# Hybrid attention and mixture-of-experts block: one flat loop of visits, quarter-form steps, the lone expert second

## The reference

```python
def _moe_ffn(h, w_router, w_gate, w_up, w_down):
    logits = h @ w_router
    top_val, top_idx = lax.top_k(logits, 2)
    gate = jax.nn.softmax(top_val, axis=-1)
    ...
    # for each token and each of its two experts e, with weights of width 3584:
    y_assign = (silu(x @ w_gate[e]) * (x @ w_up[e])) @ w_down[e]
    ...
    # the two results of a token, scaled by gate, are added up
```

## Time and profile before

| | us |
|---|---|
| median of 3 runs (1669.82 to 1673.24) | 1670.78 |
| the profiled execution | 1672.14 |
| its span on the core | 1670.4 |
| PE busy | 1544.0 (92%) |
| DVE busy | 418.1 (25%) |
| ACT busy | 250.2 (15%) |

### The profile page before, as it was taken

The page is one execution under the profiler, slowest core; times in us unless marked ns, Lnnn a source line. Parts: engine busy times, 40 slices in busy tenths (PEclk is TensorE's granted clock), DMA queues, the critical chain, the costliest instruction groups (busy, mean ns, idle before and its releaser), DMA issues.

```text
span 1670.4 us, 21757 instructions
## 1 busy us (share of the span) xinstructions
PE 1544.0 (92%) x8696; PEld 852.4 (51%) x8697; DVE 418.1 (25%) x955; ACT 250.2 (15%) x560; POOL 0.2 (0%) x4
## 2 busy tenths in 40 slices
PE   5988889999989998599999999999999999999996
PEld 2777658777657774444444443443333443333332
DVE  2366525333344533600002000110000300003003
ACT  2132210000012331110101010011111111111112
POOL 0000000000000000000000000000000000000000
PEclk8999799999999998799999999999999999999998
DMA  9974525765656440068979797999999999997991
GB/s 348 380 266 164 189 101 192 273 252 202 227 193 229 172 178 16 1 264 332 407 289 407 284 408 294 408 374 405 408 407 407 407 377 407 407 408 296 367 377 78
DMA packets 168185, 484.43 MB, mean 290 GB/s; under 512 B 10024, under 2 KB 20544, under 8 KB 168000
## 3 DMA queue, kind: packets, MB, share of 16 engines
q1 hardware_dynamic: 168128, 483.70, 75.8%
HBM read 482.63 MB, written 1.05 MB: 290 GB/s over the span
## 4 chain that ended last, share of the span: by engine, by line
PE 79%; DMA 9%; DVE 5%; SPq 3%; ACT 2%; issue 2%; DVEq 0%; ACTq 0%
PE bank L1024 11%; PE bank L931 9%; PE bank L1064 8%; DMA ring<-in_w_exp_up 8%; PE bank L778 7%; PE bank L1008 6%; PE bank L1185 6%; PE bank L1020 5%; PE bank L949 4%; PE bank L912 4%; PE bank L1058 3%; PE bank L1211 3%; PE bank L772 3%; SPq L629 2%; PE bank L1280 2%
## 5 line engine op out<-in xcount | busy, mean ns | idle before, releaser
L1024 PE MATMUL bank<-ring,hT 128*64 128x448 f32 x1280 | 255.1, 546 | 32.2 <-DMA ring<-in_w_exp_up 12.7
L1024 PEld LDWEIGHTS bank<-ring,hT 128*64 128x64 f32 x1280 | 89.0, 137 | 190.7 <-issue 153.7
L931 PE MATMUL bank<-hT,ring 128*128 128x256 f32 x704 | 158.0, 385 | 1.7 <-DVE hT L1429 1.7
L778 PE MATMUL bank<-hT,ring 128*128 128x256 f32 x640 | 153.0, 396 | 3.9 <-ACT hT L1953 2.5
L1809 DVE TENSOR_TENSOR bt<-arena,bank 64x512 f32<-64x512 f32 (+2 forms) x36 | 24.3, 675 | 493.5 <-PE bank L1024 249.6
L931 PEld LDWEIGHTS bank<-hT,ring 128*128 128x128 f32 x704 | 135.2, 193 | 24.1 <-issue 3.8
L778 PEld LDWEIGHTS bank<-hT,ring 128*128 128x128 f32 x640 | 124.5, 198 | 26.0 <-DVE hT L1429 4.4
L1064 PE MATMUL bank<-ring,bt 128*32 128x256 f32 (+1 forms) x1232 | 136.8, 445 | 0.0
L1348 DVE SCALAR_TENSOR_TENSOR acc<-ring,cond,acc 128x512 f32<-128x512 f32 x140 | 105.2, 752 | 4.9
L1020 PE MATMUL bank<-ring,hT 128*128 128x448 f32 x256 | 100.7, 546 | 4.1 <-DMA ring<-in_w_exp_up 3.4
L1008 PE MATMUL bank<-ring,hT 128*32 128x448 f32 x1024 | 102.8, 542 | 0.0
(11 more groups left out here) (279 smaller groups left out, 1179.8 us busy)
## 6 DMA issues: line engine op xcount, KB each, us to landing
ring<-in_w_exp_gate SPq DMA_DIRECT2D x128, 896.0 KB, 9.2
ring<-in_w_exp_up SPq DMA_DIRECT2D x128, 896.0 KB, 13.0
ring<-in_w_exp_down SPq DMA_DIRECT2D x64, 1536.0 KB, 15.9
ring<-in_w_ada SPq DMA_DIRECT2D x24, 2048.0 KB, 9.4
ring<-in_w_in SPq DMA_DIRECT2D x10, 2048.0 KB, 12.8
ring<-in_w_exp_down SPq DMA_DIRECT2D x32, 512.0 KB, 16.3
ring<-in_w_ff_gate SPq DMA_DIRECT2D x5, 2048.0 KB, 12.4
ring<-in_w_ff_up SPq DMA_DIRECT2D x5, 2048.0 KB, 12.8
```

The source lines that it names most:

```text
L778: last = mm(o[:, 0:T], w[:, k, t * P:(t + 1) * P], hT[:, k, :], start=(k == 0), stop=(k == KC - 1))
L931: last = mm(bank[n % 2][:, a * T:(a + 1) * T], w[a][:, k, t * P:(t + 1) * P], hT[:, k, :], start=(k == 0), stop=(k == KC - 1))
L1024: last = mm(o[64 * c2:64 * c2 + 64, 64 * c2:64 * c2 + EH], xsT[:, k, t0:t0 + 64], w[:, k, c2 * EH:(c2 + 1) * EH], start=(k == 0), stop=(k ...
```

## The change

Seven edits:

- **One loop.** The nested loops become one of NV = 21 visits. A visit is at most one small job, at most one large job behind it, and perhaps an end. Each engine reads five values per visit from the constant table (`job_at`, `ends_seen`, `has_small`, `large_no`, `end_of`), and inside the visit the class of its small or large expert.
- **Tiny steps.** A class 0 of up to 32 tokens (`TINY`). A small step of this class is one quarter unit: 32 matmuls for gate and up together, whose pieces are released as they are used; then Silu, product, four transposes and 28 down matmuls.
- **Order.** The smallest rank goes to position 2, and `LONE = 1`: the second large expert is the one alone. Jobs 0 to 11 keep their pattern, jobs 12 to 15 are `(3,0)` to `(3,3)`, then four pairs `(6,s) (5,s)` and four pairs `(8,s) (7,s)`.
- **Start.** Only the first half of the gather stands ahead of the loop. The second half, the first large window, the clearing of `ys`, `yacc` and banks 4 to 6, and the transposes of the scatter weights form an "end 3" behind job 0.
- **Scatter.** The first scatter (behind job 5) uses both tiles instead of one.
- **Small outputs.** For a class 0 expert the output is copied by four copies of 32 rows, two on each engine, instead of two of 64 rows, and DVE and ACT read the class for it.
- **Routing.** One more DVE instruction for the class, one that keeps the class of the other path at 1 or above.

The visits are (number of the job, small, large, end): `0 s end3; 1 L; 2 s; 3 s+L; 5 s end1; 6 s+L; 8 s; 9 s+L; 11 s end2; 12 L; 13 L; 14 L; 15 L end2; 16, 18, 20 s+L; 22 s+L end2; 24, 26, 28 s+L; 30 s+L end2`.

```diff
-STREAM_AT = (0, 1, 3, 5, 7, 2, 4, 6)
+STREAM_AT = (0, 1, 3, 5, 7, 6, 8, 2)
 NPOS = 16
-LONE = 3
+LONE = 1
 JOBS = []
 for l_ in range(4):
     for s_ in range(ES):
-        small_ = {0: 2 * (s_ // 2), 1: 4, 2: 6}.get(l_)
+        small_ = {0: 2 * (s_ // 2), 2: 6, 3: 8}.get(l_)
         if l_ != LONE:
             JOBS.append((small_, 2 * s_ % ES if l_ == 0 else s_))
         JOBS.append((2 * l_ + 1, s_))
         if l_ == 0:
             JOBS.append((small_, 2 * s_ % ES + 1))
-AHEAD_OF_LARGE = [n - 1 for n, (pos_, _) in enumerate(JOBS) if pos_ % 2]
-ENDS_SEEN = [0, 0, 1, 1] + [2] * 4 + [3] * 4 + [4] * 4
-JOBS_DONE = [12, 20, 28, 32]
+JOBS_DONE = [12, 16, 24, 32]
+VISITS = []
+small_left, ends_, j_ = ES, 0, 0
+while j_ < len(JOBS):
+    has_, large_ = JOBS[j_][0] % 2 == 0, 0
+    visit_ = [j_, ends_, int(has_), 0, 0]
+    j_ += has_
+    small_left -= has_
+    end_ = 3 if has_ and j_ == 1 else int(has_ and ends_ == 0 and small_left == 0)
+    end_ = 2 if has_ and j_ in JOBS_DONE else end_
+    if not end_ and j_ < len(JOBS) and JOBS[j_][0] % 2:
+        visit_[3] = JOBS[j_][0] // 2 + 1
+        j_ += 1
+    if not end_ and (j_ == len(JOBS) or j_ in JOBS_DONE):
+        end_ = 2
+    visit_[4] = end_
+    ends_ += end_ in (1, 2)
+    VISITS.append(visit_)
+NV = len(VISITS)
+PLAN = [v[0] for v in VISITS] + [len(JOBS)] + [v[k] for k in range(1, 5) for v in VISITS]
+NPLAN = len(PLAN)
+C_END = C_PLAN + NPLAN
 TX = 3 * P // 2
+SECOND_BANKS = (4, 5, 6, 1)
...
+TINY = 32
+UNITS = {0: [("quarter", 0)], 1: [("half", 0)], 2: [("half", 0), ("quarter", 64)], 3: [("wide", 0), ("quarter", 128)],
...
+        def large_class(eng, no):
+            return eng.value_load(route_i.rearrange("p a r -> p (a r)")[0:1, bass.ds(2 * no + 4 * NPOS - 1, 1)], min_val=0, max_val=4)
+
+        def planned(eng, at, u, most):
+            return eng.value_load(plan_i[0:1, bass.ds(u + at, 1)], min_val=0, max_val=most)
+
+        def job_at(eng, u):
+            return planned(eng, 0, u, 32)
+
+        def ends_seen(eng, u):
+            return planned(eng, NV + 1, u, 4)
+
+        def has_small(eng, u):
+            return planned(eng, 2 * NV + 1, u, 1)
+
+        def large_no(eng, u):
+            return planned(eng, 3 * NV + 1, u, 4)
+
+        def end_of(eng, u):
+            return planned(eng, 4 * NV + 1, u, 3)
...
-            for h in range(2):
+            def gather(h, banks):
+
                 pe.wait_ge(sel_v, 2 + h)
                 for k in range(KC):
                     for b in range(2):
-                        last = mm(bank[4 * h + k // 2][:, k % 2 * T:(k % 2 + 1) * T], xn[:, b, k * P:(k + 1) * P],
+                        last = mm(bank[banks[k // 2]][:, k % 2 * T:(k % 2 + 1) * T], xn[:, b, k * P:(k + 1) * P],
                                   sel[:, b, h * T:(h + 1) * T], start=(b == 0), stop=(b == 1))
                     if k % 2:
                         last.then_inc(gat_p, 1)
+
+            gather(0, range(4))
...
-            def quarter(t0, ks):
+            def quarter(t0, ks, alone=False):
 
                 for k in ks:
                     for q, w in enumerate((eg, eg, eu, eu)):
@@ -1009,6 +1043,8 @@
                                   w[:, k, (q % 2) * EH:(q % 2 + 1) * EH], start=(k == 0), stop=(k == KC - 1))
                         if k % 2 and q % 2:
                             last.then_inc(u_used if q == 3 else g_used, 1)
+                        elif alone and k == KC - 2 and q % 2:
+                            last.then_inc(eu_p if q == 3 else eg_p, 3)
...
+            def tiny_step(J, ends):
+
+                pe.wait_ge(xsS_v, ends + 1)
+                pe.wait_ge(yacc_v, 4 * ends + 12)
+                for k in range(0, KC, 2):
+                    pe.wait_ge(full_g[k // 2], 16 * J + 16)
+                    pe.wait_ge(full_u[k // 2], 16 * J + 16)
+                    quarter(TX, range(k, k + 2), True)
+                pe.wait_ge(yzS_v, ends + 1)
+                pe.wait_ge(eh_v, 4 * J + 4)
+                h, one_ = hs[64:P, 0, :], ident[64:P, 64:P]
+                mm(bank[3][:, 0:64], h[:, 0:P], one_, start=True, stop=True)
+                for t in range(1, 4):
+                    last = nc.tensor.transpose(bank[3][:, t * 64:(t + 1) * 64], h[:, t * P:(t + 1) * P], one_)
+                last.then_inc(et_p, 4)
+                down(J, 0, 0, ALL, (0,), 7)
...
-                pe.wait_ge(xsS_v, 1)
-                turn_scatter_weights(0, bank[3])
-                with nc.Fori(0, 4, engines=PE, head_slot={PE[0]: 0}) as l:
-                    which = class_at(pe, 2 * l + 1)
-                    with pe.Fori(0, ES) as i:
-                        J = job_ahead(pe, l, i)
-                        ends = ends_seen(pe, l, i)
-                        with pe.If(l != LONE):
+                with nc.Fori(0, NV, engines=PE, head_slot={PE[0]: 0}) as u:
+                    J, ends, has, large, end = (f(pe, u) for f in (job_at, ends_seen, has_small, large_no, end_of))
+                    with pe.If(has != 0):
+                        tiny = class_at(pe, 2 * ends)
+                        with pe.If(tiny == 0):
+                            tiny_step(J, ends)
+                        with pe.Else():
                             small_step(J, ends)
+                    with pe.If(large != 0):
+                        which = large_class(pe, large)
                         with pe.If(which == 3):
-                            large_step(l, J + 1, ends, 3)
+                            large_step(large, J + has, ends, 3)
                         with pe.Else():
-                            large_step(l, J + 1, ends, 2)
-                        with pe.If(l == 0):
-                            small_step(J + 2, ends)
-                            with pe.If(i == 1):
-                                stream_scatter(0, (1,))
-                    stream_scatter(l + 1, (0, 1))
+                            large_step(large, J + has, ends, 2)
+                    with pe.If(end != 0):
+                        with pe.If(end == 3):
+                            gather(1, SECOND_BANKS)
+                            turn_scatter_weights(0, bank[0])
+                            pe.wait_ge(sgt_a, 1)
+                        with pe.Else():
+                            stream_scatter(ends, (0, 1))
             with pe.Else():
+                gather(1, range(4, 8))
                 with nc.Fori(0, NE, engines=PE, head_slot={PE[0]: 0}) as r:
                     pe.wait_ge(xsT_v, r + 1)
                     which = class_of(pe, r)
@@ -1656,8 +1713,8 @@
                 signal(ins, sel_v)
 
...
-            then(ts(total, sums, float(CAPS[0]), 1.0, ALU.is_gt, ALU.add))
-            for cap in CAPS[1:]:
+            then(ts(total, sums, float(TINY), None, ALU.is_gt))
+            for cap in CAPS:
...
+                with ve.If(class_at(ve, 2 * g) == 0):
+                    for c in (2, 3):
+                        last = nc.vector.tensor_copy(ys[64:96, 1, c * T:(c + 1) * T], bank[7][32 * c:32 * c + 32, 0:T])
+                    last.then_inc(ys_v, 1)
+                with ve.Else():
+                    nc.vector.tensor_copy(ys[64:P, 1, CW:D], bank[7][64:P, :]).then_inc(ys_v, 1)
...
-                stream_weights(0)
                 gathered(0)
                 small_window(None)
-                gathered(1)
-                large_window(1)
-                ve.wait_ge(sgt_p, 1)
-                stream_weights(1)
-                signal(nc.vector.memset(ys, 0.0), dv)
-                nc.vector.tensor_copy(yacc, xs[:, :, :]).then_inc(yacc_v, 4 * NE + 1 - 20)
-                for i in (4, 5, 6):
-                    last = nc.vector.memset(bank[i][:, :], 0.0)
-                last.then_inc(yzL_v, 1)
-                ve.wait_ge(sgt_a, 1)
-                nc.vector.memset(bank[7][:, :], 0.0).then_inc(yzS_v, 1)
-                with ve.Fori(0, 4) as l:
-                    which = class_at(ve, 2 * l + 1)
-                    with ve.Fori(0, ES) as i:
-                        J = job_ahead(ve, l, i)
-                        with ve.If(l != LONE):
+                nc.vector.memset(bank[7][:, 0:T], 0.0).then_inc(yacc_v, 4 * NE + 1 - 20)
+                nc.vector.memset(bank[7][:, T:], 0.0).then_inc(yzS_v, 1)
+                with ve.Fori(0, NV) as u:
+                    J, ends, has, large, end = (f(ve, u) for f in (job_at, ends_seen, has_small, large_no, end_of))
+                    with ve.If(has != 0):
+                        with ve.If(class_at(ve, 2 * ends) == 0):
+                            stream_step(J, 0)
+                        with ve.Else():
                             stream_step(J, 1)
-                        with ve.If(which == 3):
-                            stream_step(J + 1, 3)
+                    with ve.If(large != 0):
+                        with ve.If(large_class(ve, large) == 3):
+                            stream_step(J + has, 3)
                         with ve.Else():
-                            stream_step(J + 1, 2)
```

(24 more changed lines are left out.)

73 lines of the change are left out of this document (38 added, 35 removed).

## The result

The changed kernel takes 1709.8 us (median of 4, 1708.3 to 1710.2) where the kernel before, on the same chip, took 1670.6: the ratio is 1.023, 95% interval 1.0213 to 1.0248. The forecast was 1680, at most 1693. The span grew by 37.5 us, from 1670.4 to 1707.9.

The account below looks back on a forecast made before the run. It took the weight DMAs to bound the paired jobs and triples, PE the lone jobs. Terms +1.3 (start), -1.5 (triples), 0 and +9.6 (from J=12) gave +9.4: median 1670.8 to 1680 us, range 1664 to 1693.

Parts of the forecast that it names:

- two signs of being wrong: A first large step before 726 us, or lone intervals under 31.5, would make the forecast wrong.
- triples, J2 to J11: Three groups of two small jobs and one three-unit large job: 92.6 us each by first gate issues; -1.5 taken.
- J11 to the start of J=12: From job 11's first gate issue to PE's start of job 12: 51.1 us against 51.2, so nothing.
- Start: First large step at 731 us (bounds 725 and 737), job 2's first gate issue at 758.0: +1.3.
- rival of instruction fetch: Jumps miss at each visit, 3.6 us bare of 6.02: +27 on top, 1707; chance 0.06.
- The gap: PE idle between a large step and the next visit, from register loads and branches: 4.0 us, bounds 0.74 and 5.
- A tiny step's stall: PE's wait between a tiny step's gate/up and down matmuls: 4.35 us of 14.4, bounds 3.1 to 5.
- From J=12 on: Job 12's start to the last step's end: three lone intervals of 33.5 us, fourteen DMA-bound jobs 376.55; +9.6.
- The clock rival: Idle gaps may drop PE to 1.2 GHz, 1.6 us per gap: +10.4 on top, 1690; chance 0.17.
- The rival of hidden loads: The queue hides the register loads, gap stays 0.74 us: 1667.0, or 1661 with a start at 725; chance 0.28.
- The tiny form: If not taken, PE needs 103 us in the triple with the scatter, about +10 more; chance 0.02.

Follow-up runs that it names:

- e4: The changed kernel with visit 0 written out ahead of the loop, which starts at 1: 1693.0 us.
- e6: The changed kernel with the edits of e3 and e4 together: 1672.3 us.
- e8: The kernel of e6 with the large step first in a visit and the small or tiny one behind it: 1664.6 us.
- e3: The changed kernel with the five plan values of a visit packed in one word, split by divisions and remainders, on all three engines: 1684.3 us.
- e11: The kernel before with four more register reads (values zero) on TensorE at the head of each inner round: 1693.9 us.
- e2: The changed kernel with TINY = 0, so every small expert takes the small step of before: 1729.5 us.
- e7: The kernel of e6 with TINY = 0, small steps in place of all tiny ones: 1689.4 us.
- e12: The changed kernel with one Silu of one column on ScalarE ahead of its loop: 1707.4 us.
- e13: The kernel before with one Silu of one column on ScalarE ahead of its loop: 1669.5 us.

## Why the prediction was wrong

The direction held, and so did one mechanism, reads of the plan that leave PE bare. The sum for the profiled execution was +9.4 and the span grew 37.5. Neither of its two signs of being wrong came: the first large step started at 736.86 and no lone interval was under 33. What is missing, by its own steps (28.1 in all but for rounding):

| step | forecast | measured | missing |
|---|---|---|---|
| ahead of the gather, untouched | 0 | -4.6 | -4.6 |
| from the gather to J2 | +1.3 | +13.7 | 12.4 |
| triples, J2 to J11 | -1.5 | +11.7 | 13.2 |
| J11 to the start of J=12 | 0 | +2.9 | 2.9 |
| from there to the last step's end | +9.6 | +13.6 | 4.0 |
| behind it | 0 | +0.3 | 0.3 |

- **Start: the failed step, a term mis-sized.** "The row of 6.02 us for a single branch shows what the first jump over a large step costs; I add half of it, 3, and take 731." In its place stand four long jumps of 3.9, 7.5, 6.0 and 5.8 us, 23.2 in all. Counted from the first gather J=0 started as forecast (13.4 us behind it, 13.5 in my sum), but the second gather 11.7 later than in it: I had priced "branches over both large steps (1.4)" at the ordinary rate, where PE was idle for 9.5, and J=0 took 18.1 for 14.4. With the first large step at the lower clock J2 is then 13.7 late, beyond my bound of +7. The second pair of jumps falls on J=2, which I had put under the triples at nothing: 12.0 us between J2 and J5 (105.8, before 93.8). Together the four jumps and what came with them are some 24 us of what is missing.
- **The rival of instruction fetch** named long jumps, with the wrong condition: I asked whether they are long at every visit. They are long only in the first two visits, and that is dear there, where the next loads hang on them. Its 1707 lies near the measured 1709.8 by luck: it was made of long jumps at every lone step and pair, of which none came. That the long branches are fetches is read from their place and from e4, e6 and e8, where they go with the jumps; no run shows a fetch itself, nor why some first jumps are short (over tiny and small step together at 735.3, 0.22; over the three-unit step alone at 1109.0, 0.21). The Trainium skill, page Runtime: NRT & Kernel Launch, section Instruction fetch mechanics, says that a taken branch out of the window waits for a fetch. The four long branches fit that; the later jumps over the same code, 0.22 at most, show nothing of the kind.
- **The gap**: 4.0 forecast, 3.70 measured; e3 and e11 confirm the price of the reads from both sides.
- **A tiny step's stall**: 4.35 forecast, 4.56 measured (1089.91 to 1094.47). The step took 17.9 for 14.4, since its matmuls took 7.90 and 5.49 for 6.43 and 3.64. Within the triples this is hidden, as forecast (92.6 and 93.1 for 92.6); between J11 and J=12 it is not, 2.9.
- **From J=12 on**: the lone intervals were 33.3, 36.1 and 35.0 for 33.5, together 3.8 more, and the gate issue in the one that follows came 1.5 late; the small expert's pairs took 54.4, where I had let them fit under 53.8, and J17 to J31 1.5 more than the 376.55; the last step ended 3.1 earlier than my 51.0. (My terms add up to 570.8, not 570.7.)
- **The clock rival** was thus half right, beside the forecast rather than in its place. Its 1.6 us per gap was near (1.4 to 2.9 behind lone gaps), and it costs where PE sets the end: 6.0 in three lone steps (2.8, 1.7, 1.5), 3.3 in the last tiny step before J=12, 1.9 in the first large step. That is 11.2, where I had 10.4 as a case by itself with a chance of 0.17; J=0's own matmuls took 13.6 for 10.1 besides.
- **The rival of hidden loads** was wrong: the gap is 3.70, and e11 has it without the flat loop.
- **The tiny form** brings 17 to 20 us, where I had priced its absence at about 10, in the triple with the scatter. There it brings 12.5 in e2 and 5.0 in e7; the rest comes from J11 to PE's start of J=12 (3.5 and 7.6), from the start in e7, and, only with the large gaps of e2, from the pairs (6.6). The gaps are thus a part of the reason and not all of it.

## What to carry to other kernels

A loop whose body is chosen by table pays on the sequencer of the engine that bounds it: count the register reads in a round, pack them into one word, and place the code so that the first pass skips nothing large. Price each first jump over code, not one; such a jump counts most where the pipeline of loads is being filled, because all later work starts that much later. A saving on an engine that the transfers hide comes back into view when other edits open gaps on it: small steps in the pairs cost 6.6 us with gaps of 3.7 and nothing with gaps of 1.3. And before two profiles are compared stretch by stretch, take a common start behind the part that the change leaves alone.

## What the runs showed of the hardware

- Four jumps in the first two passes over TensorE's loop took 3.9 to 7.5 us and the branch that left it 3.4; all other branches of that loop took at most 0.33.
- A register read on TensorE's sequencer cost 0.78 us of bare time (3.1 for four), for 0.31 in the profile's record. Divisions and remainders on a read word cost far less: e3's gap is 1.3 with one word split five ways, where four reads fewer alone would leave 0.6 of the 3.7, so by that estimate the splitting costs 0.7.
- Behind 2.8 us of idle a quarter's matmuls took 7.92 us in e12 and 6.22 in e4: the length of the idle alone doesn't tell whether the clock falls.
- One Silu ahead of a loop took 28 (e13) or 38 (e12) table loads of 1.28 us out of it, and changed the time by 0.9 to 2.4 us, within the uncertainty.
